# A chunk's scan products on TensorE, moved from between its two halves to behind its weight products and their signal

## The reference

```python
def prep(a):                       # a: normed and modulated tokens, context and latent
    q, v, g = jnp.split(a @ w_in, [2048, 4096], axis=-1)
    z = jnp.clip(jnp.einsum('bld,wdk->wblk', a, w_f), -30, 30)    # w: two directions
    log_f = jax.nn.log_sigmoid(z) + jnp.log1p(lb * jnp.exp(-z))
    k = (1.0 - lb) * jax.nn.sigmoid(-z)
    q = jax.nn.silu(q) * 128 ** -0.5
...
# per head and direction: S_t = diag(f_t) S_{t-1} + k_t v_t^T,  o_t = S_t^T q_t
# the context is scanned first, its last state starts the latent scan
y = (rms_norm(o_forward + o_backward) * silu(g)) @ w_o
h = x + m[2] * y
h = h + m[5] * ((silu(t @ w_gate) * (t @ w_up)) @ w_down)     # t: h normed, modulated
out = rms_norm(h)
```

## Time and profile before

| | |
|---|---|
| median of 3 runs | 1943.01 us (1941.77 to 1945.99) |
| profiled execution | 1942.41 us, of which 1940.1 us span from first to last instruction |
| PE, PEld busy | 1852.1 us (95%), 1689.8 us (87%) |
| DVE, ACT busy | 1256.8 us (65%), 861.9 us (44%) |
| chunks 16 to 127 (VQ, Z with scans) | 205.94 to 901.10 us |
| chunks 128 to 159 (G with scans) | 901.10 to 1047.81 us |
| mean granted clock of TensorE | 0.99 |

### The profile page before, as it was taken

One profiled execution on the slowest core, in us unless ns is written; L12 is line 12 of the kernel. 1 busy time (PEld: TensorE's weight loads), 2 busy tenths in 40 slices (PEclk: granted clock), 3 DMA queues, 4 the chain that ended last, 5 costly groups with the idle time before them and its releaser, 6 DMA issues.

```text
span 1940.1 us, 31876 instructions
## 1 busy us (share of the span) xinstructions
PE 1852.1 (95%) x13318; PEld 1689.8 (87%) x13318; DVE 1256.8 (65%) x1949; ACT 861.9 (44%) x1186; POOL 0.2 (0%) x4
## 2 busy tenths in 40 slices
PE   6989999999999999999889999999999999999998
PEld 2258989788989788888779989999999999999996
DVE  4754768686968787878985455555545555545445
ACT  4582535343545344545445454333333433444444
POOL 0000000000000000000000000000000000000000
PEclk9999999999999999999999999999999999999999
DMA  8965544443444444443655546777767676555552
GB/s 326 392 217 167 170 128 138 141 153 125 147 131 131 157 147 130 142 141 120 196 185 209 183 123 206 216 227 217 217 218 218 214 225 212 182 182 183 182 185 98
DMA packets 175377, 353.18 MB, mean 182 GB/s; under 512 B 12737, under 2 KB 80642, under 8 KB 174594
## 3 DMA queue, kind: packets, MB, share of 16 engines
q1 hardware_dynamic: 175042, 351.11, 56.2%
q10 hardware_dynamic: 192, 0.05, 0.0%
HBM read 346.92 MB, written 4.19 MB: 181 GB/s over the span
## 4 chain that ended last, share of the span: by engine, by line
PE 79%; DVE 14%; DMA 2%; issue 2%; ACT 2%; ACTq 0%; DVEq 0%
PE bank L1122 19%; PE bank L1123 19%; PE bank L1124 19%; DVE wlo L689 3%; DVE aacc L783 3%; PE score L1227 2%; PE bank L1159 2%; PE bank L1161 2%; PE bank L1160 2%; DMA raw<-in_w_ada_dram 2%; PE score L1122 1%; PE score L1123 1%; PE score L1124 1%; DVE work L867 1%; DVE work L837 1%
## 5 line engine op out<-in xcount | busy, mean ns | idle before, releaser
L1122 PE MATMUL bank<-ahi,whi 128*128 128x256 f32 (+1 forms) x2912 | 891.8, 306 | 34.7 <-DVE wlo L689 19.0
L1123 PE MATMUL bank<-alo,whi 128*128 128x256 f32 (+1 forms) x2912 | 882.7, 303 | 0.0
L1124 PE MATMUL bank<-ahi,wlo 128*128 128x256 f32 (+1 forms) x2912 | 882.4, 303 | 0.0
L689 DVE TENSOR_TENSOR wlo<-raw,whi 128x1024 fp32r<-128x1024 f32 x496 | 605.7, 1223 | 417.6 <-ACT whi L426 417.0
L426 ACT ACTIVATE whi<-raw 128x1024 fp32r<-128x1024 f32 x496 | 522.3, 1056 | 547.8 <-PE bank L1124 447.1
L1122 PEld LDWEIGHTS bank<-ahi,whi 128*128 128x128 f32 x2912 | 560.3, 192 | 63.8 <-DVE wlo L689 22.7
L1124 PEld LDWEIGHTS bank<-ahi,wlo 128*128 128x128 f32 x2912 | 560.3, 192 | 20.7
L1123 PEld LDWEIGHTS bank<-alo,whi 128*128 128x128 f32 x2912 | 560.6, 193 | 18.5
L1159 PE MATMUL bank<-whi,ahi 128*128 128x256 f32 x512 | 151.1, 295 | 16.0 <-DVE arena L793 9.9
L783 DVE SCALAR_TENSOR_TENSOR aacc<-raw,cs,aacc 128x1024 f32<-128x1024 f32 x120 | 153.5, 1279 | 0.5
L1161 PE MATMUL bank<-whi,alo 128*128 128x256 f32 x512 | 146.2, 285 | 0.0
(11 more groups left out here) (216 smaller groups left out, 1780.7 us busy)
## 6 DMA issues: line engine op xcount, KB each, us to landing
raw<-in_w_ada_dram SPq DMA_DIRECT2D x168, 512.0 KB, 3.9
raw<-in_ffn_w_gate_dram SPq DMA_DIRECT2D x88, 512.0 KB, 3.8
raw<-in_ffn_w_up_dram SPq DMA_DIRECT2D x88, 512.0 KB, 4.1
raw<-in_ffn_w_down_dram SPq DMA_DIRECT2D x88, 512.0 KB, 3.4
raw<-in_hg_w_in_dram SPq DMA_DIRECT2D x128, 256.0 KB, 3.1
raw<-in_hg_w_f_dram SPq DMA_DIRECT2D x128, 256.0 KB, 3.5
raw<-in_hg_w_in_dram SPq DMA_DIRECT2D x32, 512.0 KB, 4.6
raw<-in_hg_w_o_dram SPq DMA_DIRECT2D x32, 512.0 KB, 3.6
```

The costliest lines, as they stand in the source:

```text
L689: dve.tensor_tensor(wlo[:, ck % SPL, :], raw[:, SEQ["w", ck] % RAW, :], whi[:, ck % SPL, :].bitcast(F32), ALU.subtract).then_inc(s_lo, 1)
L1122: pe.matmul(dst, w, ah, start=start, stop=False, skip_group_check=True)
L1123: pe.matmul(dst, w, al, start=False, stop=False, skip_group_check=True)
L1124: return pe.matmul(dst, wl, ah, start=False, stop=stop, skip_group_check=True)
```

## The change

In `chunk()`, the calls of `scan` and `sum_modulation` leave the place between the halves and stand behind the loop, after the signal `s_used` of the chunk's last product. `turn_rows(pe, 3)`, which belongs to the first chunk only, stays between the halves.

```diff
--- before.py
+++ after.py
@@ -1127,13 +1127,8 @@
 
                 s = ck % SPL
                 for a in range(2):
-                    if a:
-                        for j, n in between:
-                            scan(j, n)
-                        for e in ada_ends(ck):
-                            sum_modulation(e)
-                        if ck == C_B:
-                            turn_rows(pe, 3)
+                    if a and ck == C_B:
+                        turn_rows(pe, 3)
                     k = 2 * r + a
                     first, end = k == 0, k == KD - 1
                     if ck < C_B + 8 and kind == "VQ":
@@ -1182,6 +1177,10 @@
                             last = three(bank[bb + f // 2][:, (f % 2) * T:(f % 2 + 1) * T], whi[:, s, o], wlo[:, s, o],
                                          ahi[:, k, tk], alo[:, k, tk], first and f % 2 == 0, end)
                 last.then_inc(s_used, 1)
+                for j, n in between:
+                    scan(j, n)
+                for e in ada_ends(ck):
+                    sum_modulation(e)
 
             def wide(ck, i, half, k_end, frees):
```

## The result

The changed kernel takes 1995.33 us (median of 4 runs, 1991.41 to 1997.41) against 1943.88 for the kernel before beside it (4 runs, 1941.77 to 1945.99): the ratio is 1.0258, interval 1.0242 to 1.0273. The forecast was 1988 with a range of 1965 to 2010. It is slower by 51.5 us, 5.8 more than the sum of 45.7. The profiled execution took 1993.9 us in all.

The account below looks back on a forecast made before the run. The bound was taken as a loop passing between PE and DVE once a head, neither engine full. (a) 19.0 + 13.0 - 0.7, (b) 4.3, (c) 2.8, (d) 4.3, (f) 3 sum to 45.7 us; on 1942.4 that is 1988, range 1965 to 2010.

Parts of the forecast that it names:

- (a): Task 8 releases `ksum` half a chunk late: 19.0 us in Z chunks, 13.0 in VQ chunks, less 0.7 at the clip.
- (b): First placing (L863) released late: nothing in VQ and Z chunks; with `ksum`'s delay 4.3 us in G chunks (1.4 to 5.8).
- (d): ACT gets task 10's mean square (`s_om`) late, delaying later chunks' high and low halves: 4.3 us, bounds 0 and 13.
- (c): Modulation sums end later in chunks 54 and 102, so DVE waits: 2.8 us in all, bounds 0 and 4.3.
- (e): Earlier `s_used` frees ACT's copy and PE's wait inside task 9, but gains nothing; bounds 0 to 13 us of gain.
- (f): Longer PE pauses after task 8 lower the granted clock: 3 us, from heads 4, 10, 12; bounds 0 and 20.
- D: Rival, chance 0.19: each of 13 heads gets a slow-clock stretch, and ACT's delays come at twice the size: 2007 us.
- A: Rival, chance 0.05: earlier `s_used` shortens PE's waits for the low half, about 13 us less, 1929 us.
- B: Rival, chance 0.05: no change, DVE catches the 2.7 us up in room after `ksum`: 1942 us.
- C: Rival, chance 0.24: only (a) holds; (b), (c), (d) and (f) vanish in overlooked room: 31 us, 1974 us.

## Why the prediction was right, and where it was not

**(a)** Right, in place and size. Over the thirteen chunks behind a task 8, the steps sum to 30.0 us (2.8 in five Z chunks, 1.9 in the two of heads 0 and 6, 2.2 or 1.9 in the VQ chunks), and some 2.5 us follow one or two chunks later, where the step behind the chunk was short; 31.3 was forecast. The time from `ksum` to PE's restart at the clip or the values was not 15.9 us in all heads, as the prediction's sign has it, but 16.4 to 19.1 by head; in each it is the same in the changed kernel within 0.3, but for heads 3 and 9 with their sums. Task 8 alone gives 38.8, and all the others 18.6.

One thing that was to show it was wrong: L863's wait was to stay near 67 us or fall, and it rose to 93.4. DVE's work is the same and the loop is longer, so the time has to stand somewhere on DVE. In the changed kernel the tasks 6 and 8 are late by the same, DVE meets task 6 first, and most of the added wait is put down there; where only task 8 is late, it is put down at L896 (71.5 against 37.2). The mechanism was right, the row by which I meant to know it was not.

**(b)** Nearly right outside the G chunks: with task 6 alone behind, the six VQ heads lose 0.25 us each, so the 2.3 to 2.4 us of room counted there were a little too many, and the Z heads lose nothing. In the G stage 6.9 us were lost in all, against 4.3 here and 1.2 of (d), which falls at chunk 129. DVE waits longer in both places of head 14 than in the earlier trace rows (1.82 and 0.66):

```profile
1014.56 0.29 DVE L863 TENSOR_TENSOR work<-score,ident 128x128 f32<-128x128 f32 x1 [3.10 <-PE score L1229]
...
1024.69 0.42 DVE L896 TENSOR_TENSOR work<-arena 128x256 f32<-128x256 f32 x1 [1.98 <-PE score L1229]
```

Each is up by 1.3 us, of 1.2 and 1.4 forecast.

**(c)** Right: 1.35 us in each of heads 3 and 9, of 1.4 forecast. That PE would start chunk 54 earlier after `ksum` than before was part of the working, and it is why the sum costs less here than by itself. Chunk 54 and its sum, against the earlier trace rows:

```profile
448.20 0.39 PE L1237 MATMUL ob<-work,arena 128*128 128x128 f32 x2
...
449.54 1.84 PE L1256 MATMUL bank<-ones,aacc 128*128 128x1 f32 x16
...
451.42 0.17 DVE L950 TENSOR_TENSOR mod<-bank,bias 128x8 f32<-128x8 f32 x1 [1.46 <-PE bank L1256]
```

**(d)** The sum was right and its parts were not quite. ACT's way, against the earlier trace rows:

```profile
515.22 0.47 ACT L575 ACTIVATE rstd<-mx,eps 128x256 f32<-128x256 f32 x1 [3.18 <-PE mx L1244]
...
523.25 1.05 ACT L426 ACTIVATE whi<-raw 128x1024 fp32r<-128x1024 f32 x1
...
524.34 1.22 DVE L689 TENSOR_TENSOR wlo<-raw,whi 128x1024 fp32r<-128x1024 f32 x1
...
525.61 0.39 PE L1154 MATMUL bank<-whi,ahi 128*128 128x256 f32 x1 [0.69 <-DVE wlo L689]
```

From chunk 64 to chunk 66 it is 9.55 us, before 8.71. With the 0.47 us one chunk on, head 4 costs 1.3 (1.1 forecast); head 10 0.85 (0.6), head 12 1.3 (1.2), head 5 1.1 (0.7), head 11 nothing that can be seen (0.7): 4.6 against 4.3. What was overlooked: the high half of the chunk ahead of the clip also comes late through task 9, and DVE's lo with it (0.20 us in chunk 63). In heads 0 and 6 the way from `ksum` to the clip is 0.3 us longer by that; in heads 4, 10 and 12 it takes the 0.25 us that the prediction had counted as given back. Against the sum that is 1.3 us.

**(e)** Right: nothing came back, and the kernel that gives the earlier signal up is the faster one.

**(f)** The size was right by luck. Three heads, 4, 10 and 12, were to have a slow stretch with 60% chance each. Their pause came as forecast (2.85 us ahead of chunks 62, 110 and 126), and behind none of them did the clock fall. Windows of a pause and of what followed it, ahead of chunk 38 (head 1) in the first two rows and of chunk 62 (head 4) in the last two:

```profile
332.90:336.20 3.30, 0.45 (x5) 0.26 (x3) 2.87 (x4) 0.85 (x1) 0.00 (x0) 1.00 0.13 19
337.00:340.40 3.40, 3.40 (x18) 3.40 (x18) 3.16 (x11) 0.00 (x0) 0.00 (x0) 0.50 0.71 248
499.30:502.20 2.90, 0.07 (x1) 0.00 (x0) 2.79 (x4) 0.00 (x0) 0.00 (x0) 1.00 0.04 5
502.20:509.10 6.90, 6.88 (x37) 5.92 (x37) 6.62 (x19) 0.00 (x0) 0.00 (x0) 1.00 0.49 155
```

Two pauses of one length (PE idle for 2.85 us in each), and behind one the granted clock is 0.50, behind the other 1.00. Nor is it the place: in the kernel with task 8 alone behind, the pauses are the same, and behind those ahead of chunks 94, 110 and 126 the clock did fall. There, ahead of chunk 110 and behind it:

```profile
813.35:816.25 2.90, 0.05 (x2) 0.03 (x1) 2.84 (x4) 0.00 (x0) 0.00 (x0) 0.99 0.04 8
816.25:819.65 3.40, 3.40 (x8) 2.72 (x9) 3.12 (x11) 0.00 (x0) 0.00 (x0) 0.50 0.90 285
```

In the changed kernel the clock fell to the lower of its levels behind pauses at chunks 32, 38, 48, 56, 80, 86, 96, 104 and 120: 30.7 us of the scan stage at half clock, before 17.1. A stretch of 3.41 us cost about 1.5 us (chunk 32 took 5.88 us instead of 4.39), but nothing at chunks 38 and 86, which took 7.4 us as before, because PE's waits of 1.25 us inside them are gone: that DVE's lead would swallow the slow stretches of heads 1 and 7 was right. What chunks lost by the clock in the scan stage is some 7.7 us in the changed kernel that the one before didn't lose, and 4.2 us in the one before (behind chunks 48 and 88) that the changed one didn't: net 3.5. That is the 3 of the sum, but by other heads than the three that it named, less two slow stretches of the kernel before, so the agreement is luck. In the G stage 13.6 us are at half clock, before 10.2, which is at most 1.7 us. "More than ten dips, then D holds" was a bad test: counted in stretches of 3.41 us there are thirteen in the scan and G stages against eight before, and what they cost more is a third of D's 18 us at most.

In the scan stage it adds up: 32.5 (a) + 2.7 (c) + 3.3 (d, without chunk 129) + 0.6 (the clips of heads 0 and 6) + 3.5 (clock) = 42.6, of 42.4 measured. The 5.8 us by which the sum fell short in the profiled execution (51.5 against 45.7) are 2.2 ahead of the stage, 1.4 in the G stage, and 2.2 in the scan stage, of which 1.3 at the clips. The 2.2 ahead of the stage come in the 40 chunks ahead of C_B (3.4 us more, less 1.2 in the first chunk behind it), where the two kernels are the same, with 6.8 us at half clock in either profile; what made them is not shown, and they are not the change's.

**The rivals.** A falls by the kernel with the tasks ahead of the last group. B falls by the result. C (1974) falls, since (c) and (d) are measured. D is refuted in its size: the changed kernel has 13.6 us more at half clock in the scan stage and 3.4 more in the G stage, which at half speed is 8.5 us at the most. What the sum had right above all is that it went by the loop, and not by the busy shares of the page, in which neither engine is full.

Left open: why some pauses of 2.85 us are followed by the lower clock and others, as long and as empty, are not.

## What to carry to other kernels

When two engines pass work to each other once a tile, and neither is full, write down the loop: what A does from B's signal to its own, and what B does from there. A signal on the path of that loop, moved behind independent work, adds that work's length to every round in full, though no instruction is added (here task 8); one with room behind it costs next to nothing (task 6, 0.25 us in six of the heads). Moving a signal ahead gains only what the other engine had stood still for. A late signal can show at another wait than its own, one that the engine meets earlier, so know its cost by the length of the loop and by where PE starts its chunks, not by the wait that you expect to grow; and look whether a second small buffer takes the signal out of the loop.

## What the runs showed of the hardware

A part of the single microseconds between two profiles is the clock and not the change. Over all 29 runs of the kernel before that ran beside these kernels, the mean granted clock lies between 0.988 and 0.993, and the time falls by some 1.2 us for each 0.001 of it (correlation -0.74). In ten of the twelve experiments' profiles a stretch at half clock of 3.4 or 6.8 us began within or behind PE's pause ahead of the values in chunk 40 (2.85 us long in eight of the ten); in the profiles of the kernel before and of the changed kernel, with the same pause, the clock stayed at 1.00. Where the pause was of that length, the stretch made chunk 40 1.6 us longer or more, and that stands in the comparison with the profile of the kernel before. The Trainium skill ("TensorE: Matmul & The Clock Gate", section "What's actually happening") calls the slower clock the default that activity lifts. Here the five pauses of 2.85 us ahead of the Z chunks 46, 62, 94, 110 and 126 of the changed kernel, with PE idle all through them, were each followed by a clock of 1.00, and with task 8 alone behind the last three of the same five by 0.50. Pauses of 1.8 us ahead of chunks 32 and 80 of the changed kernel were followed by 0.50 too. So a pause of 1.8 to 2.85 us makes the slow clock possible and not certain.
